# Convolution, head norms and rotation of a mixer block moved beside its input projection, in a two-block network on one core

## The reference

```python
def _token_mixers(h, hc, w_in_l, q_norm, k_norm, rpb, lb_fwd, lb_bwd, hg_norm_l, conv_w_l, rope_cos, rope_sin, need_ctx):
    p = jnp.split(jnp.einsum('btd,dk->btk', h, w_in_l), pts, axis=-1)
    pc = jnp.split(jnp.einsum('btd,dk->btk', hc, w_in_l), pts, axis=-1)
    q = _rope(_rmsnorm(na_heads(p[0]), q_norm), rope_cos, rope_sin)
    k = _rope(_rmsnorm(na_heads(p[1]), k_norm), rope_cos, rope_sin)
    na = _na_latent(q, k, v, kc, vc, rpb).reshape(b, n, NA_DIM)
    hg, hg_c = _hgrn2_mixer(p[3:8], pc[3:8], lb_fwd, lb_bwd, hg_norm_l, need_ctx)
    cv = _short_gated_conv(p[8], p[9], p[10], conv_w_l)

def _rope(x, cos, sin):
    return x * cos + _rot(x) * sin

def _short_gated_conv(b_gate, c_gate, u, w):
    z = c_gate * u
    y = sum(w[j] * zp[:, j:j + t] for j in range(CONV_WIDTH))
    return b_gate * y
```

## Time and profile before

| what | value |
|---|---|
| median of 3 runs | 4321.2 us (4318.56 to 4324.83) |
| the profiled execution | 4321.0 us, its span 4318.9 us |
| PE busy | 3748.0 us, 87% of the span |
| DVE busy | 2422.0 us, 56% |
| ACT busy | 1782.9 us, 41% |
| POOL busy | 311.9 us, 7% |
| chain that ended last, by engine | PE 76%, DVE 9%, ACT 7%, issue 2%, DMA 2% |

### The profile page before, as it was taken

How to read it: one execution, slowest core, us unless ns; L and a number is a source line. 1 busy time by engine, 2 the same in 40 slices (tenths; PEclk the granted TensorE clock), 3 DMA queues, 4 the chain that set the end, 5 groups by cost and what they waited for, 6 DMA issues and landing times.

```text
span 4318.9 us, 52752 instructions
## 1 busy us (share of the span) xinstructions
PE 3748.0 (87%) x19820; PEld 2887.6 (67%) x19820; DVE 2422.0 (56%) x3543; ACT 1782.9 (41%) x2871; POOL 311.9 (7%) x384
## 2 busy tenths in 40 slices
PE   1996687799799658699899998799999999879998
PEld 1885456566588335455688776678777887647876
DVE  5764773688583675698577334666433332464332
ACT  2113653589522564488422133632233222353222
POOL 1100001110110000100022000011000000000000
PEclk9998858899899856799999999999999999999999
DMA  6542001699464101499488331057423223302222
GB/s 221 179 160 65 1 31 39 215 362 357 159 227 132 35 1 59 163 366 360 165 275 269 102 101 56 15 186 238 161 96 117 95 98 98 146 1 89 97 93 73
DMA packets 185550, 615.86 MB, mean 143 GB/s; under 512 B 39897, under 2 KB 42585, under 8 KB 184041
## 3 DMA queue, kind: packets, MB, share of 16 engines
q1 hardware_dynamic: 117808, 430.62, 28.5%
q0 software_dynamic: 39072, 141.58, 10.1%
q10 hardware_dynamic: 28442, 40.50, 3.0%
HBM read 596.33 MB, written 18.02 MB: 142 GB/s over the span
## 4 chain that ended last, share of the span: by engine, by line
PE 76%; DVE 9%; ACT 7%; issue 2%; DMA 2%; POOL 1%; ACTq 1%; POOLq 0%; DVEq 0%; SPq 0%
PE psum L1998 21%; PE psum L733 11%; PE psum L2011 11%; PE psum L1772 8%; PE psum L800 4%; PE psum L1791 4%; PE psum L666 3%; PE psum L863 3%; POOL spare L566 1%; DVE spare L1129 1%; PE psum L1026 1%; PE psum L1036 1%; ACT PB L1085 1%; PE psum L672 1%; DMA rel_rows<-H 1%
## 5 line engine op out<-in xcount | busy, mean ns | idle before, releaser
L692 DVE TENSOR_TENSOR ring_r<-ring,small_r 128x1024 fp32r<-128x1024 f32 x280 | 344.5, 1234 | 853.9 <-ACT small_r L688 853.7
L688 ACT CAST small_r<-ring 128x1024 fp32r<-128x1024 f32 x280 | 292.6, 1049 | 1194.3 <-PE psum L733 342.4
L688 ACT CAST PB_r<-ring 128x1024 fp32r<-128x1024 f32 x328 | 341.8, 1053 | 542.3 <-PE psum L1998 327.3
L692 DVE TENSOR_TENSOR ring_r<-ring,PB_r 128x1024 fp32r<-128x1024 f32 x328 | 394.6, 1222 | 218.3 <-ACT PB_r L688 217.4
L1998 PE MATMUL psum<-H_r,ring_r 128*128 128x512 f32 x1344 | 332.9, 390 | 0.0
L1998 PE MATMUL psum<-H_r,small_r 128*128 128x512 f32 x1344 | 326.8, 395 | 0.0
L1998 PE MATMUL psum<-H_r,PB_r 128*128 128x512 f32 x1344 | 318.3, 389 | 0.0
L1998 PEld LDWEIGHTS psum<-H_r,small_r 128*128 128x128 f32 x1344 | 252.4, 188 | 60.3
L1998 PEld LDWEIGHTS psum<-H_r,ring_r 128*128 128x128 f32 x1344 | 252.3, 188 | 53.9
L1998 PEld LDWEIGHTS psum<-H_r,PB_r 128*128 128x128 f32 x1344 | 252.3, 188 | 52.4
L733 PE MATMUL psum<-H_r,small_r 128*128 128x512 f32 (+1 forms) x1040 | 273.4, 366 | 5.7 <-issue 5.7
(11 more groups left out here) (380 smaller groups left out, 6965.9 us busy)
## 6 DMA issues: line engine op xcount, KB each, us to landing
ring<-wtile SPq DMA_DIRECT2D x800, 512.0 KB, 5.1
spare<-wmod POOLq DMA_DIRECT2D x97, 512.0 KB, 4.9
H<-wmod POOLq DMA_DIRECT2D x48, 512.0 KB, 3.7
PB<-wmod POOLq DMA_DIRECT2D x48, 512.0 KB, 3.7
X<-wmod POOLq DMA_DIRECT2D x47, 512.0 KB, 5.0
PB<-wmod SPq DMA_DIRECT2D x8, 1024.0 KB, 23.6
X<-x_in ACTq DMA_DIRECT2D x2, 3072.0 KB, 11.3
X<-rpb_rows ACTq DMA_DIRECT2D x24, 224.0 KB, 5.0
```

Of the source, the lines that this page charges most:

```text
L688: nc.scalar.copy(high(j), slot(g0 + j)).then_inc(high_ready.sem, 1)
L692: nc.vector.tensor_tensor(low(g0 + j), slot(g0 + j), high(j).bitcast(F32), ALU.subtract).then_inc(low_ready.sem, 1)
```

## The change

1. The convolution, and the squares, sums, Ln, Exp and scaling of the head norms, leave their stage and run inside `project`, in a new class `InputTiles`: the convolution in DVE's steps 6 to 15, one head norm at every second step from 8 on (ACT squares at 8, 10, ..., PE sums behind tile 9, 11, ..., 19, ACT's Ln and Exp and DVE's scaling at step 10, 12, ..., 20).
2. The rotation matrix is gone. ACT copies the normed Q and K with each group of 16 partitions exchanged with its neighbour (8 DMAs from SBUF to SBUF, 1.57 MB in all), and DVE multiplies and adds during tiles 4 to 6 of `project_rows` (`rotate`).
3. The bias tables are built on the host with the mask in them, 0.92 MB for a pair of heads; one is loaded at the start of the rows, two at their end (`fetch`, `move`). `rpb_rows`, its 12 DMAs at the start, the 24 loads of bias tables and POOL's masking are gone.
4. `project_rows` is flowing: the row tiles are split by the same `weights` as the tiles before, the first two of them during the last two steps of `project`. PE waits for the last copies, and in the first block for all modulation jobs (`banks_free`). `qkv` and `kvw` change with it.
5. The head norms' sums use PSUM banks 4 and 5, so `condition` has one scratch area in PSUM for its first product in place of two, and each job waits for the one before it.

```diff
-            if i >= 2:
-                eng.wait_ge(mod_used.sem, base + i - 1)
+            if i >= len(junk):
...
-                for h in range(DEPTH * NA_HEADS):
-                    eng.dma_start(rpb_rows[h], bass.AP(tensor=rpb.tensor, offset=h * RPB_HEAD, ap=[[0, GRID_W], [1, RPB_ROW]])).then_inc(rpb_spread.sem, 16)
...
-                    if j + 2 < n:
+                    if j + 2 < n + more:
                         split_high(eng, j + 2)
+                    if inside is not None:
+                        inside.sca(eng, j)
...
+                    if inside is not None:
+                        inside.squares(eng, j)
...
-                    if j + 2 < n:
+                    if j + 2 < n + more:
                         split_low(eng, j + 2)
+                    if inside is not None:
+                        inside.vec(eng, j)
...
+                eng.wait_ge(act_freed.sem, freed[0])
+                eng.wait_ge(dve_freed.sem, freed[1])
+                if inside is not None:
+                    inside.banks_free(eng)
...
-                for j in range(2):
-                    split_high(eng, j)
+                if inside is not None:
+                    inside.fetch(eng)
                 for j in range(n):
                     if j + 2 < n:
-                        split_high(eng, j + 2)
+                        split_high(eng, first + j + 2)
...
+                        if inside is not None and j == n - 1:
+                            inside.move(eng)
...
-                    split_low(eng, j)
+                    if j >= 2:
+                        split_low(eng, first + j)
...
-            stage(tensor=ten, scalar=sca, vector=vec)
+                    if inside is not None and j in (4, 5, 6):
+                        inside.rotate(eng, 2 * j - 8)
+                        inside.rotate(eng, 2 * j - 7)
+            stage(flowing=True, tensor=ten, scalar=sca, vector=vec)
...
+            def ten(self, eng, j):
+                i, odd = divmod(j - 9, 2)
+                if odd or not 0 <= i < self.n:
+                    return
+                eng.wait_ge(head_squared.sem, self.b_sq + i + 1)
+                if i:
+                    eng.wait_ge(head_read.sem, self.b_read + i)
+                for a, b, w in self.items[i][2]:
+                    mm = nc.tensor.matmul(bank[4 + w][:, 0:b - a], blk, self.work(i)[:, a:b], start=True, stop=True)
+                mm.then_inc(head_summed.sem, 1)
+
+            def sca(self, eng, j):
+                i, odd = divmod(j - 10, 2)
+                if odd or not 0 <= i < self.n:
+                    return
+                work, end = self.work(i), self.items[i][2][-1][1]
+                eng.wait_ge(head_summed.sem, self.b_sum + i + 1)
+                for a, b, w in self.items[i][2]:
+                    ins = nc.scalar.activation(work[:, a:b], bank[4 + w][:, 0:b - a], ACT.Ln, bias=cn("eps", 0, 1), scale=1.0 / DH)
+                ins.then_inc(head_read.sem, 1)
+                eng.wait_ge(head_read.sem, self.b_read + i + 1)
+                nc.scalar.activation(work[:, 0:end], work[:, 0:end], ACT.Exp, scale=-0.5).then_inc(head_root.sem, 1)
+
+            def squares(self, eng, j):
+                i, odd = divmod(j - 8, 2)
+                if odd or not 0 <= i < self.n:
+                    return
+                tile, _, parts = self.items[i]
+                end = parts[-1][1]
+                eng.wait_ge(act_freed.sem, self.lat_freed(tile))
+                if len(parts) > 1:
+                    eng.wait_ge(dve_freed.sem, self.ctx_freed(tile))
+                if i >= 2:
+                    eng.wait_ge(head_scaled.sem, self.b_sc + i - 1)
+                nc.scalar.activation(self.work(i)[:, 0:end], pt(tile, 0, end), ACT.Square).then_inc(head_squared.sem, 1)
+
+            def vec(self, eng, j):
+                if 6 <= j < 16:
+                    self.conv_step(eng, *divmod(j - 6, 5))
+                i, odd = divmod(j - 10, 2)
+                if odd or not 0 <= i < self.n:
+                    return
+                tile, weight, parts = self.items[i]
+                end = parts[-1][1]
+                eng.wait_ge(head_root.sem, self.b_root + i + 1)
+                nc.vector.scalar_tensor_tensor(pt(tile, 0, end), pt(tile, 0, end), weight, self.work(i)[:, 0:end], ALU.mult, ALU.mult).then_inc(head_scaled.sem, 1)
...
+                if step == 2:
+                    for a, b, w in parts:
+                        ins = nc.vector.scalar_tensor_tensor(cc[:, a + 1:b], cu[:, a:b - 1], tap(0), cc[:, a + 1:b], ALU.mult, ALU.add)
+                    V(eng, ins)
...
+                if step == 4:
+                    nc.vector.tensor_tensor(cb[:, 0:end], cb[:, 0:end], cc[:, 0:end], ALU.mult)
...
+            def banks_free(self, eng):
+                eng.wait_ge(head_read.sem, self.b_read + self.n)
+                eng.wait_ge(mod_used.sem, self.mods_done)
+
+            def fetch(self, eng):
+                eng.wait_ge(head_scaled.sem, self.b_sc + self.n)
+                eng.wait_ge(mod_used.sem, self.mods_done)
+                eng.dma_start(ROPE, rope).then_inc(rope_loaded.sem, 16)
+                for a in range(8):
+                    b = a ^ 1
+                    eng.dma_start(TURNED[16 * a:16 * a + 16, :, :], QK[16 * b:16 * b + 16, :, 0:NLAT]).then_inc(rope_moved.sem, 16)
+                eng.dma_start(BT[0], biases[self.l, :, 0:BIAS_PAIR]).then_inc(bias_loaded[0].sem, 16)
+
+            def rotate(self, eng, i):
+                if i == 0:
+                    eng.wait_ge(rope_loaded.sem, self.rope)
+                    eng.wait_ge(rope_moved.sem, self.moved)
+                t, r = QK[:, i, 0:NLAT], TURNED[:, i, :]
+                nc.vector.tensor_tensor(r, r, ROPE[:, NLAT:2 * NLAT], ALU.mult)
+                V(eng, nc.vector.tensor_tensor(t, t, ROPE[:, 0:NLAT], ALU.mult))
+                nc.vector.tensor_tensor(t, t, r, ALU.add)
+
+            def move(self, eng):
+                for p in range(1, NA_TILES):
+                    eng.dma_start(BT[p], biases[self.l, :, p * BIAS_PAIR:(p + 1) * BIAS_PAIR]).then_inc(bias_loaded[p].sem, 16)
+                    if p == 1:
+                        end = self.end
+                        eng.dma_start(Hv[:, 6:8, 0:end], PB[:, T_CB * NTOK:(T_CB + 2) * NTOK].rearrange("p (k t) -> p k t", k=2)[:, :, 0:end]).then_inc(conv_moved.sem, 16)
...
-        def mask_biases(eng, loaded_count):
-            win = cn("win", 0, GRID_W).unsqueeze(1).broadcast_to([P, 14, GRID_W])
-            eng.wait_ge(bias_loaded.sem, loaded_count)
-            for h in range(NA_HEADS):
-                nc.gpsimd.tensor_tensor(BT[:, h, :, :], BT[:, h, :, :], win, ALU.add)
...
+            inside = InputTiles(l, need_ctx, mod_used.count)
+            freed = project(f"win_{l}", 0, N_PT, WIDE, dest(IN_ORDER), [need_ctx or j not in n_ctx_free for j in range(N_PT)],
...
+            project_rows(f"win_{l}", N_PT, 2, NA_DIM, WIDE, lambda c, t: (VN, VI)[c][:, t, :], TT, weights, freed, None, inside)
             if upto <= 5: break
-            attention(neighbourhood() + (context_attention() if need_ctx else []), SN, EN, rb[:, 0:256], [(0, 1, 2, 3)])
+            attention(neighbourhood(l) + (context_attention() if need_ctx else []), SN, EN, rb[:, 0:256], [(0, 1, 2, 3)])
             back = x_loaded.reserve(16) + 16
             if upto <= 6: break
-            recurrence(l, need_ctx, lambda eng, l=l: eng.dma_start(X[:, :], x_save if l else x_in).then_inc(x_loaded.sem, 16))
...
```

More of the change, by code:

```diff
@@ L33 @@
 RPB_R, RPB_C = 2 * NA_ROWS - 1, 2 * NA_COLS - 1
[L34 to L36 removed]
+BIAS_ROWS = 14
+BIAS_PAIR = HEADS_PER_TILE * BIAS_ROWS * GRID_W
 CHUNK = 128
@@ L262, in build @@
         x_saved, x_loaded = sig("x_saved"), sig("x_loaded")
-        rope_loaded, bias_loaded = sig("rope_loaded"), sig("bias_loaded")
+        rope_loaded, rope_moved, conv_moved = sig("rope_loaded"), sig("rope_moved"), sig("conv_moved")
+        bias_loaded = [sig(f"bias_loaded{p}") for p in range(NA_TILES)]
+        head_scaled = sig("head_scaled")
         mod_in = [sig(f"mod_in{b}") for b in range(4)]
@@ L705, in weight_parts, with project @@
             return split_high, split_low, passes, halves
-        def project(name, first, n, src, dest, with_ctx, scale=1.0, weights=None, normed=None, beside=None, form=None, loads=None, needs=None):
+        def project(name, first, n, src, dest, with_ctx, scale=1.0, weights=None, normed=None, beside=None, form=None, loads=None, needs=None, inside=None, more=0):
             g0 = FIRST[name] + first
@@ L717, in project @@
             split_high, split_low, passes, _ = weights or weight_parts(g0, n)
+            if inside is not None:
+                inside.follow(lambda j: fa + j + 1, lambda j: fv + n_ctx[j] + 1)
             def ten(eng):
@@ L735, in ten @@
                     mm.then_inc(tile_used, 1)
+                    if inside is not None:
+                        inside.ten(eng, j)
                 if needs is not None:
```

(31 more changed lines are left out.)

204 lines of the change are left out of this document (84 added, 120 removed).

## The result

The changed kernel takes **4257.5 us** (median of 4 runs, 4251.1 to 4262.4) against 4322.2 (median of 4, the three of the table above and one more): a ratio of 0.985, 95% interval 0.9833 to 0.9867. Forecast were 4250 us, within 4233 to 4274.

The account below looks back on a forecast made before the run. PE bounds projections and rows; between rows and attention a serial chain stands on the path. Layer 0's -31.1, layer 1's -33.9, the start's -4 and `qkv`/`kvw`'s -2.5 sum to -71.5: 4250 us, range 4233 to 4274.

Parts of the forecast that it names:

- the two stretches: From the rows' end to attention's first matmul, 50.50 and 48.53 us before: they nearly vanish, -46.0 and -44.0 us.
- `qkv` and `kvw`: Start of these rows: PE waits only for the last copy, 0.60 us, instead of 2.03 and 1.70; -2.5 us together.
- The three issues: ACT's DMA issues ahead of its last six copies after the rows: 0.5 us each, bounds 0.3 and 1.11.
- Layer 0's projection: PE gains six head sums of 1.41 us, and step 20 adds a stall; +9.0 us, 8 to 12.
- the stall of step 20: Layer 0's projection: no head sum follows this norm step, so PE stalls 0 to 1 us, taken as 0.5.
- Layer 0's pause: Between projection and rows: PE waits for DVE's split and last jobs, 7.0 us instead of 2.30; +4.7 us.
- Layer 1, up to tile 11: Projection with DVE already behind: job waits of 0.12 us, ten times, and four convolution steps; +4.0 us, 2.7 to 7.
- The rival of the bending projections: Both projections: each job's wait for the one before costs 0.5 instead of 0.12 us; 4257 us, chance 0.08.
- Layer 1, the other tiles: Projection from tile 11 on: PE leads again and adds the other five head sums; +6.1 us.
- The exchange: Q and K copies during the rows: free if landed by 33 us after the rows' start; some 15 us expected.
- The rival of 43 GB/s: Exchange lands 44 us after the rows' start, so PE stalls 11 us per layer; 4272 us, chance 0.12.
- The start: Kernel start: twelve DMAs, 1.7 MB, gone from the engines that load the constants; -4 us, 0 to -8.

Follow-up runs that it names:

- bankwise: The changed kernel with PE's first row matmuls waiting for each PSUM bank separately instead of for all copies and modulation jobs; 4247.9 us, ratio 0.9847.
- convlate: The changed kernel with layer 1's ten convolution steps in DVE steps 12 to 21 instead of 6 to 15; 4251.9 us, ratio 0.9857.
- best: The changed kernel with bank by bank waits, row tile 2's cast ahead of ACT's DMA issues, and layer 1's convolution in steps 12 to 21; 4231.7 us.
- exchlate: The changed kernel with the exchange and its neighbouring loads issued after the copies of the rows' first half, both layers; 4284.1 us, ratio 0.9927.
- again: The changed kernel itself, unaltered, run once more as a base for variants; 4254.0 us, ratio 0.9867.
- spreadback: The changed kernel with the twelve 64-row writes put back at the start, their result unused; 4260.2 us, ratio 0.9875.
- conswide: The changed kernel with 192 unused columns put back into the constants; 4259.5 us, ratio 0.9871.

## Why the prediction was right

The measured median lies 7.5 us above the forecast and inside the range. The gain came where it was forecast, in the two stretches, and most of the costs by the mechanisms named; one step failed (`qkv` and `kvw`), and one term was sized a third too small.

**The two stretches.** -46.0 and -44.0 were forecast, -46.4 and -44.1 came. The three issues took 0.33, 0.57 and 0.61 us, 0.50 in the mean, as taken.

**Layer 0's projection.** +9.0 both, by parts that err against each other: a head sum takes 1.29 us with its 768 tokens and not 1.41, so six make 7.7; the stall of step 20, taken as 0.5, is 0.77; the last 0.5 are small waits and losses of clock. That both come to +9.0 is luck.

**Layer 0's pause.** 7.40 us, forecast 7.0, released by L379 as said; bankwise shows that it was this wait: with it gone the rows start 0.26 us after the projection. The rows' first half lost less clock than taken: 27.22 us for 28.0.

**Layer 1, up to tile 11.** The mechanism held, 62.35 us of DVE against 57.7. Of the 4.6, the convolution is 2.8, as forecast, and convlate and best take just that out of DVE's course. The wait of a job for the one before is 0.18 us and not 0.12. The rival of the bending projections, at 0.5, fell.

**Layer 1, the other tiles.** This term was off by most: +9.6 for +6.1. Five sums are 0.86 or 1.29 us each, 5.6 in all. Two items were missing. Tile 22 waits 1.40 us, until 1319.72, for DVE's context copy of step 20, which starts at 1319.19 and takes 0.42; it is the stall that the forecast had only for layer 0; tile 21 has no context in layer 1 and is short, so the copy is wanted sooner. And tile 11 takes 2.6 us longer after its wait, because the clock was lower. The forecast had priced clock after a pause at the rows, from the earlier trace rows, and not at this wait, which it knew to grow.

**The exchange.** It landed by 20 us after the rows' start, and 33 was the latest that would do; exchlate confirms the 33. The rival of 43 GB/s fell: 1.57 MB landed within 20 us, though from partitions in groups of 16. The Trainium skill, page "SBUF — State Buffer", section "Door 1: The DMA port swizzle", measures 104 GB/s for partitions 0 to 15, which gives an estimate of 15 us for the 1.57 MB. The trace is near that and does not contradict it: from the first issue at 320.13 to the last landing lie 14 to 19 us, 8 of them ACT's issues. Those took 1.02 us each, as bounded by the old tables' 1.11.

**The start.** -3.0 for -4, by the writes that ran beside the constants, as spreadback and conswide show. The same start in again was 1.5 us shorter still (89.47), so the size is known to a microsecond or two only.

**`qkv` and `kvw`.** -0.5 for -2.5, a failed step: "PE waits for that copy alone, 0.60". The last tile's copy stands in ACT behind the cast of the next weights, which the joined rows brought there:

```profile
2547.86 1.04 ACT small_r L687
2548.90 0.51 ACTq L330
2549.41 0.04 issue
2549.45 6.78 PE psum L814 x28
```

1.65 us, then, and nearly the old pause. For layer 0 the forecast had that cast in its sum, here not.

**Outside the mixer.** The forecast named a stage outside that moves by over 3 us as a sign of error. The end of layer 0's recurrence did, by 4.2, and convlate, which is the same up to there, did not have them; the stretch behind it moved by 2.7, and by 4.0 between after and again, which are one program. Everything outside the terms makes 4.7 of the 10.7 us between the forecast span and the measured one; the terms explain the other 6.0.

## What to carry to other kernels

When a wait is known to grow, price the clock behind it too, and not at the stage's end alone; take a range, since here a wait of 2.2 us cost 1.7 us of clock at one tile and 0.2 at another. A wait for "everything of the stage before" deserves to be split by what each instruction really needs; behind it there may be a second wait in another engine's order (here ACT's DMA issues ahead of a cast), and then most of the gain comes only with both, 17 us here against 6 for the first alone. Moved work is free until an in-order engine's sum up to the next copy reaches PE's: sum that engine's steps from where it fell behind, and place the work after that point.

## What was not expected of the hardware

- Kernels that are the same up to there ran the 147 matmuls of the recurrence's end in 12 or in 17 us of PE's time, at a granted clock of 0.72 or 0.50, a stretch of 22.96 or 27.15 us; two variants had a third length, 18.6. Some 450 us before the end after gained 2.6 us in this way (clock 0.93 and 0.77 in before, 1.00 and 0.88 in after).
- Two waits of PE of 2.16 and 2.17 us in the same projection: behind one the clock stayed at 1.00, behind the other it was 0.83 in the mean over the next 10.22 us.
- Twelve DMA writes of 2244-byte rows, 1.7 MB, made a load of constants beside them some 3 to 4 us longer (24.05 to 24.51 us in the eleven traces without, 27.55 and 28.07 with them), while a seventh more columns in the load cost nothing that shows.
